# Gated linear attention on Trainium2: the first weight chunk takes its place in the load ring ahead of the two gate matrices

## What is computed

```python
def swiglu(x, w_in, w_out):
    gate, up = jnp.split(x @ w_in, 2, axis=-1)
    return (jax.nn.silu(gate) * up) @ w_out

def gla_attention(x, w_in, w_gate2, b_gate, norm_g, w_o):
    ...
    q, k, v, g_out, g_low = jnp.split(x @ w_in, splits, axis=-1)
    log_alpha = jax.nn.log_sigmoid((g_low @ w_gate2 + b_gate).astype(jnp.float32)) / GLA_GATE_TEMP
    ...
for layer in range(DEPTH):
    g = norm_g[layer]
    ff = swiglu(rmsnorm(h, g[0]), ffn_w_in[layer, 0], ffn_w_out[layer, 0])
    h = h + 0.5 * rmsnorm(ff, g[1])
    u = rmsnorm(h, g[2])
    ...
    h = h + rmsnorm(m, g[3])
```

## Time and profile before

| | us |
|---|---|
| median of 3 runs | 3548.35 |
| lowest, highest | 3547.12, 3551.14 |
| the profiled execution, own time | 3546.63 |
| its span in the trace | 3545.0 |
| PE busy | 3299.9 (93%) |
| PE weight load busy | 2901.3 (82%) |
| DVE busy | 1969.8 (56%) |
| ACT busy | 1521.4 (43%) |
| POOL busy | 192.1 (5%) |
| loads: moved, mean rate | 521.99 MB, 147 GB/s |

### The profile page before, as it was taken

How to read it: one execution, slowest core, us unless ns; L and a number is a source line. 1 busy time by engine, 2 the same in 40 slices (tenths; PEclk the granted TensorE clock), 3 DMA queues, 4 the chain that set the end, 5 groups by cost and what they waited for, 6 DMA issues and landing times.

```text
span 3545.0 us, 49189 instructions
## 1 busy us (share of the span) xinstructions
PE 3299.9 (93%) x21094; PEld 2901.3 (82%) x21094; DVE 1969.8 (56%) x2959; ACT 1521.4 (43%) x2562; POOL 192.1 (5%) x218
## 2 busy tenths in 40 slices
PE   6998999979999989899999999989989999799897
PEld 6987998967898978586989888977877887687797
DVE  4456545548555555564555565554455556625676
ACT  3455444445444433113444454444534343324453
POOL 0000000003000001320000000000011000000100
PEclk9999999989999999899999999999999999899999
DMA  6563656544656543415565536531032334431352
GB/s 219 192 199 106 210 190 201 192 137 161 220 179 215 187 140 103 143 43 173 190 196 191 190 112 219 179 103 36 16 107 95 107 107 154 129 98 48 124 186 95
DMA packets 411222, 521.99 MB, mean 147 GB/s; under 512 B 41559, under 2 KB 353484, under 8 KB 410876
## 3 DMA queue, kind: packets, MB, share of 16 engines
q1 hardware_dynamic: 405964, 516.23, 44.4%
q0 software_dynamic: 816, 2.10, 0.2%
q10 hardware_dynamic: 4224, 0.52, 0.1%
HBM read 516.19 MB, written 2.10 MB: 146 GB/s over the span
## 4 chain that ended last, share of the span: by engine, by line
PE 84%; DVE 8%; ACT 3%; DMA 1%; issue 1%; POOL 1%; SPq 0%; POOLq 0%; DVEq 0%; ACTq 0%
PE ps L186 23%; PE ps L187 23%; PE ps L188 23%; PE ps L178 4%; PE ps L196 2%; PE ps L1225 2%; PE ps L558 1%; ACT a L1245 1%; DVE small L1282 1%; POOL junk L2907 1%; PE ps L3558 0%; PE ps L3555 0%; DVE a L2421 0%; DVE tmp L645 0%; DVE a L715 0%
## 5 line engine op out<-in xcount | busy, mean ns | idle before, releaser
L186 PE MATMUL ps<-a 128*128 128x256 f32 (+1 forms) x4816 | 1526.2, 317 | 37.5 <-DVE a L715 11.5
L188 PE MATMUL ps<-a 128*128 128x256 f32 (+1 forms) x4648 | 1463.7, 315 | 0.0
L187 PE MATMUL ps<-a 128*128 128x256 f32 (+1 forms) x4520 | 1430.1, 316 | 0.0
L186 PEld LDWEIGHTS ps<-a 128*128 128x128 f32 x4816 | 927.2, 193 | 104.9 <-DVE a L715 14.1
L188 PEld LDWEIGHTS ps<-a 128*128 128x128 f32 x4648 | 894.4, 192 | 53.5
L187 PEld LDWEIGHTS ps<-a 128*128 128x128 f32 x4520 | 870.5, 193 | 51.5
L891 DVE TENSOR_TENSOR a<-ring,a 128x1024 fp32r<-128x1024 f32 x594 | 693.5, 1221 | 354.4 <-ACT a L885 354.4
L885 ACT ACTIVATE a<-ring 128x1024 fp32r<-128x1024 f32 x594 | 585.7, 1048 | 252.2 <-PE ps L188 226.2
L989 ACT ACTIVATE tmp<-ps 128x256 f32<-128x256 f32 x176 | 67.8, 385 | 508.6 <-PE ps L188 508.6
L995 DVE TENSOR_TENSOR a<-tmp,ps 128x256 f32<-128x256 f32 x176 | 74.2, 421 | 301.1 <-ACT tmp L989 301.1
L616 POOL TENSOR_TENSOR small<-small,cst 128x1 f32<-128x1 f32 (+1 forms) x78 | 52.3, 672 | 2884.6 <-DVE small L611 1997.6
(11 more groups left out here) (384 smaller groups left out, 3965.7 us busy)
## 6 DMA issues: line engine op xcount, KB each, us to landing
ring<-in_ffn_w_in_dram SPq DMA_DIRECT2D x220, 1024.0 KB, 7.3
ring<-in_ffn_w_out_dram SPq DMA_DIRECT2D x121, 1024.0 KB, 5.0
ring<-in_ada_w_dram SPq DMA_DIRECT2D x48, 1024.0 KB, 5.4
ring<-in_swa_w_qkv_dram SPq DMA_DIRECT2D x12, 1024.0 KB, 7.9
ring<-in_gla_w_in_dram SPq DMA_DIRECT2D x12, 1024.0 KB, 5.2
ring<-in_rwkv_w_rkv_dram SPq DMA_DIRECT2D x12, 1024.0 KB, 5.1
ring<-in_na_w_qkv_dram SPq DMA_DIRECT2D x12, 1024.0 KB, 5.3
ring<-in_swa_w_o_dram SPq DMA_DIRECT2D x8, 1024.0 KB, 5.5
```

The costliest lines, as they stand in the source:

```text
L186: pe.x.matmul(out, lh, rh, start=start and i == 0, stop=False)
L187: pe.x.matmul(out, lh, rl, start=False, stop=False)
L188: ins = pe.x.matmul(out, ll, rh, start=False, stop=stop and i == n - 1)
```

## The change

Among the loads that SP issues for `gla`, the first chunk of 256 columns (w0) is put ahead of `gl` and `wg`. The other three follow where all four stood. As slots are taken in turn, w0 takes the slot that `gl` had, `gl` that of `wg`, and `wg` that of w0. No load is added or left out, and the streams of the other engines are the same.

```diff
 def sp_gla(K, sp, M, f):
     tag, w, s = M.tag, M.w, K.s
+    sp_splitA(K, sp, M.S, 0, w, 0, 256)
     load_cols(K, sp, (tag, "gl"), w, 3072, 16, 8, (s.pe, (tag, "gl")))
     c = K.w.take((tag, "wg"), 1, (s.pe, (tag, "z", 1)))
     vacant(sp, c)
     sp.x.dma_start(c.buf[0:16, 0:512], K.I["gla_w_gate2"][0]).then_inc(c.sem, 16)
     load_row(K, sp, (tag, "bg"), K.I["gla_b_gate"][0], 512, (s.dve, (tag, "z", 1)))
-    sp_splitA(K, sp, M.S, 0, w, 0, D)
+    sp_splitA(K, sp, M.S, 2, w, 256, D - 256)
     load_row(K, sp, (tag, "ng"), K.I["gla_norm_g"][0], 256, (s.pool, (tag, "gain", 1, 3)))
```

## The result

The changed kernel took 3530.36 us (median of 4 runs, 3523.01 to 3531.99) against 3549.74 for the kernel before (median of 4, 3547.12 to 3551.41). The ratio is 0.9942, with a 95% interval of 0.9925 to 0.9959: faster, by 14.6 to 26.6 us. The ratio is formed over all the runs and isn't that of the medians, so the two can lie a few us apart: the medians differ by 19.4 us here, the ratio says 20.6. The forecast was 3532.7, in a range of 3529.0 to 3537.5.

A forecast was written before the change was run, and what follows sets the result against it. PE, the chain for 84% of the span, stood idle between f2 and gla while ACT waited 13.0 us for w0's late load. The wait's 13.1 us plus 2.5 of clock, other terms 0, took 3548.35 to 3532.7 us, range 3529.0 to 3537.5.

The forecast's parts named there:

- Rival (c): At ACT's L348 after f2: PE's last product, not the load, ends the wait; no change, 3548 us; chance 0.04.
- (d): At w4 in gla: the new wait stops ACT and PE; slower, measurable loss at 3555.5 us; chance 0.02.
- Part 1: SP's queue at the end of f2: w0 issued 16.8 us earlier, landing in 8.3 us, 1.1 us in time.
- Part 2: L951 to L602, f2 into gla: gain 15.62 us, 13.1 to the first L628 and 2.5 from PE's clock.
- Part 3: Product with gl opening gla: 0 put, with bounds of a gain of 1.6 us and a loss of 0.5.
- Part 4: Loads of gla that move back: all put at 0 cost, with 5.2 us kept for a late w4.
- The sum: Whole kernel: 15.6 us off the median of 3548.35 gives 3532.7 us; chance 0.78.
- Rival (a): Passage f2 to gla: only the wait goes, PE's clock still falls; gain 13.1 us, 3535.3 us; chance 0.10.
- Rival (b): Loads w0 or w4 in gla: one takes the longest landing; gain 10.4 us, 3537.9 us; chance 0.06.

The follow-up runs named there:

- the run with w4's wait alone: Kernel before, with slots of gl and wg given back only when PE has used both halves of w0, w0 still late: 3548.71 us, ratio 1.0006.
- third trace: Trace of the changed kernel run a third time with no edit, compared with the kernel before: 3531.27 us, ratio 0.9957.
- run with PE kept busy: Changed kernel plus 9 unread matmuls ahead of the second block's transposes and 10 ahead of the product with gl: 3528.43 us, ratio 0.9959.
- second and third comparison: Changed kernel rerun twice without edit against the kernel before: 3533.33 us, ratio 0.9959, then 3531.27 us, ratio 0.9957.

## Why the prediction was right

**What bounded the place.** Right as told: ACT's wait was w0's landing, w0's landing was its place behind `gl` and `wg`, and the chain behind it had nothing else that was late. Rival (c) is out by the trace of after; (d) by the same trace, where w4 lands 4.2 us before it is wanted, and by the run with w4's wait alone.

**Part 1** put w0's landing 8.3 us after its issue and 1.1 us ahead of ACT; it was 7.8 and 1.6.

**Part 2** said 15.62 us from L951 to L602, from the passage of f0. The three traces gave 15.3, 15.2 and 15.6. The 13.1 of the wait came in full, and of the clock's 2.5 the first transposes and the second `ada` product (1.8) in full. The other 0.7, which the prediction did not itemise, are the transposes of the second block: 1.97 us before, 1.28 in the model. In the changed kernel they took 1.61, 1.71 and 1.25, since the clock, still 1.00 in the 2.4 us ahead of them in the first trace, fell while they ran. The model row was one execution: in the 11 traces of this study that have nothing added there, the passage of f0 takes 19.41 to 20.13 us. The 19.43 that was used stands at the short end, and the long end would have given a gain of 14.9.

**Part 3 is the mis-sized step.** I put 0 on the product with `gl`, with a loss of up to 0.5. In two of the three traces it lost 0.8: the whole product ran at the lower clock, where before its first nine steps had run at the full one. I had bounded the loss by 24 steps of 0.21, 5.0 us in place of 4.5, and left out that one step counts whole (0.37 in the chain): it took 748.80 - 743.48 = 5.3. In the third trace it took 4.3 and gained 0.2, inside the bounds. So the term is -0.8, -0.8 and +0.2 us in the three traces, and the bound of the loss was too small by 0.3. The run with PE kept busy shows that the clock is the cause: there the product takes 3.0 us.

**Part 4** put 0 on everything that moves back. The run with w4's wait alone and the one with `gl` behind the wait on PE bear that out. One reading in it was wrong: it says that no row puts a landing over 8.3 us, where the earlier trace rows has 14.6 as the longest, which is more than the 11 us of cover that it gives `gl`. `gl` itself landed in 3.5 us, so nothing came of it.

**The sum** was 15.6 us. The traces show 14.2, 14.2 and 15.45 at the end of the mixer, and the comparisons with more runs show 14.5 and 15.3 of the whole time, with intervals that reach from about 10 to 19 us. The first comparison, with four runs each, gave 20.6, and its interval reaches down to 14.6. Part of the forecast's closeness is luck: it started from a median of three runs, 3548.35, where 21 runs later gave 3545.1 and 3545.8 and 11 runs 3547.9, and the gain was put 0.2 to 1.4 us above what the traces show, which makes up for some of it. The lower end of the range is 0.1 us off its own sum (3532.7 less 1.6 and 2 is 3529.1) and the upper 0.2, which changes nothing.

**Rival (a)**, a gain of 13.1, can't be told from the forecast by the time: its ratio of 0.9963 lies inside the intervals of the second and third comparison. The traces tell it: in all three the first transposes and the second `ada` product run at the full clock. **Rival (b)**, a late landing, showed in no run of the changed kernel.

## What to carry to other kernels

In a queue that gives out slots strictly in turn, a small load that nobody needs yet costs as much as a large one: it takes a slot ahead of the wait that the urgent load then stands behind. So order loads by when they are wanted, and look which wait stands between the last free slot and the load on the path. A second passage of the same code without the wait is the best model of what is left once a wait is gone; count its whole length, since a PE that no longer stands idle can also run the next work faster (2.5 us here), and take it from more than one execution: this one's length varied by 0.7 us.

## What the runs showed of the hardware

The executions of one kernel differ by more than the few runs at the start showed: 3540.3 to 3553.2 in 21 runs of the kernel before on one chip, 3537.0 to 3552.3 in 21 on another. A part of it is the clock of PE: the same passage of the same instructions had a granted clock of 0.72 in one execution and 1.00 in another, after idle times of PE of 1.5 and 2.3 us. In the first trace of the changed kernel L951 came 6.0 us earlier than in that of the kernel before, with 7.7 us less of PE busy on the same instructions, before the change is reached at all, so two spans should be compared stretch by stretch, from a mark ahead of the change.

Unread matmuls in PE's idle gaps of about 2 us kept the clock up where it was looked at, and with them in 11 places the whole kernel was 8 us faster. They have to fit the gap: where they outlasted it by about 10 us, the kernel became 6.7 to 13.5 us slower.
